# First weight unit issued from ScalarE's queue, and the input stream loaded in five parts

## What is computed

```
def _rmsnorm(x, g):
    xf = x.astype(jnp.float32)
    y = xf * lax.rsqrt(jnp.mean(xf * xf, axis=-1, keepdims=True) + EPS)
    return (y * g.astype(jnp.float32)).astype(x.dtype)

def _swiglu(xn, w_gate, w_up, w_down):
    return (jax.nn.silu(xn @ w_gate) * (xn @ w_up)) @ w_down
...
        f = _swiglu(_rmsnorm(h, ffn1_pre_g[i]), ffn1_w_gate[i], ffn1_w_up[i], ffn1_w_down[i])
        h = h + 0.5 * _rmsnorm(f, ffn1_post_g[i])
```

## Time and profile before

| | |
|---|---|
| time, median of 3 runs | 1560.12 us (1559.92 to 1560.37) |
| time of the profiled execution | 1560.24 us |
| its span, first to last instruction | 1558.5 us |
| TensorE busy with matmuls | 1546.3 us, 99% of the span |
| VectorE, ScalarE, GpSimd busy | 755.6, 597.5, 155.6 us |
| mean granted TensorE clock | 0.999 |
| bytes moved by DMA | 145.12 MB, mean 93 GB/s |

### The profile page before, as it was taken

How to read it: one execution, slowest core, us unless ns; L and a number is a source line. 1 busy time by engine, 2 the same in 40 slices (tenths; PEclk the granted TensorE clock), 3 DMA queues, 4 the chain that set the end, 5 groups by cost and what they waited for, 6 DMA issues and landing times.

```text
span 1558.5 us, 19025 instructions
## 1 busy us (share of the span) xinstructions
PE 1546.3 (99%) x7782; PEld 1276.9 (82%) x7782; DVE 755.6 (48%) x1190; ACT 597.5 (38%) x956; POOL 155.6 (10%) x162
## 2 busy tenths in 40 slices
PE   9999999999999999999999999999999999999998
PEld 7888888888888888888888888888888877777886
DVE  6444224346546633434843423333647455667545
ACT  6233222336433333324632323223656351544335
POOL 1311000101013400100111100110100010001100
PEclk9999999999999999999999999999999999999999
DMA  5433333322323322323233333333223452121322
GB/s 171 128 95 95 102 100 95 95 95 90 95 86 90 100 82 81 95 95 108 83 95 101 101 95 95 95 95 100 90 75 86 99 113 54 43 54 49 128 81 95
DMA packets 123735, 145.12 MB, mean 93 GB/s; under 512 B 18776, under 2 KB 86496, under 8 KB 123648
## 3 DMA queue, kind: packets, MB, share of 16 engines
q1 hardware_dynamic: 122080, 138.56, 29.5%
q0 software_dynamic: 1568, 5.34, 1.3%
HBM read 141.78 MB, written 2.10 MB: 92 GB/s over the span
## 4 chain that ended last, share of the span: by engine, by line
PE 96%; DVE 2%; ACT 1%; issue 0%; DMA 0%; POOL 0%; ACTq 0%; POOLq 0%; DVEq 0%
PE G L58 87%; PE X L58 6%; PE X L61 2%; PE G L61 1%; ACT sq_t L64 0%; DVE prb L76 0%; DVE f L70 0%; ACT prb L64 0%; DMA raw<-in_w_in_dram 0%; ACT whi L64 0%; DVE xl L73 0%; DVE ptr L67 0%; DVE h L73 0%; ACT post L64 0%; DVE tmp_t L70 0%
## 5 line engine op out<-in xcount | busy, mean ns | idle before, releaser
L70 DVE TENSOR_TENSOR wlo<-raw,whi 128x1024 fp32r<-128x1024 f32 (+3 forms) x261 | 313.2, 1209 | 490.1 <-ACT whi L64 489.9
L58 PE MATMUL G<-xh,whi 128*128 128x512 f32 (+1 forms) x1168 | 455.7, 392 | 0.2 <-DVE f L70 0.2
L58 PE MATMUL G<-xl,whi 128*128 128x512 f32 (+1 forms) x1168 | 449.9, 387 | 0.2 <-DVE xl L73 0.2
L58 PE MATMUL G<-xh,wlo 128*128 128x512 f32 (+1 forms) x1168 | 449.5, 386 | 0.4 <-DVE wlo L70 0.4
L64 ACT ACTIVATE whi<-raw 128x1024 fp32r<-128x1024 f32 (+3 forms) x261 | 266.3, 1031 | 459.2 <-DMA raw<-in_ffn_w_up_dram 159.3
L58 PEld LDWEIGHTS G<-xl,whi 128*128 128x128 f32 x1168 | 219.3, 188 | 45.5 <-DVE xl L73 0.6
L58 PEld LDWEIGHTS G<-xh,whi 128*128 128x128 f32 x1168 | 219.2, 188 | 44.1 <-issue 1.4
L58 PEld LDWEIGHTS G<-xh,wlo 128*128 128x128 f32 x1168 | 219.5, 188 | 43.2 <-DVE wlo L70 0.9
L70 POOL TENSOR_TENSOR tmp_t<-tmp_t,act_t 128x512 f32<-128x512 f32 x52 | 72.3, 1392 | 612.6 <-DVE tmp_t L70 472.1
L58 PE MATMUL G<-whi,ah 128*128 128x512 f32 x320 | 124.6, 389 | 0.0
L58 PE MATMUL G<-whi,al 128*128 128x512 f32 x320 | 124.5, 389 | 0.0
(11 more groups left out here) (272 smaller groups left out, 1795.8 us busy)
## 6 DMA issues: line engine op xcount, KB each, us to landing
raw<-in_w_in_dram SPq DMA_DIRECT2D x55, 512.0 KB, 3.7
raw<-in_ffn_w_gate_dram SPq DMA_DIRECT2D x88, 256.0 KB, 2.9
raw<-in_ffn_w_up_dram SPq DMA_DIRECT2D x88, 256.0 KB, 3.1
raw<-in_ffn_w_down_dram SPq DMA_DIRECT2D x44, 512.0 KB, 3.7
raw<-in_w_in_dram SPq DMA_DIRECT2D x12, 384.0 KB, 3.2
raw<-in_w_out_a_dram SPq DMA_DIRECT2D x8, 512.0 KB, 3.8
raw<-in_w_out_b_dram SPq DMA_DIRECT2D x8, 512.0 KB, 3.7
raw<-in_w_o_dram SPq DMA_DIRECT2D x8, 512.0 KB, 3.8
```

Of the source, the lines that this page charges most:

```text
L58: return self.e.matmul(out, lhs, rhs, start=start, stop=stop) if self.e else Idle()
L70: return self.e.tensor_tensor(*a) if self.e else Idle()
```

## The change

The first weight unit's two transfers are issued by ScalarE, as the first thing it does, with a signal of their own. `x` comes in five parts: channels 0 to 127, 128 to 255, and then three of 256. SyncE issues the first part of `x` ahead of the gain rows, and the wait for that part now stands behind the gain rows. Units 1 and 2 follow the third and the fourth part. TensorE transposes block 1 after the first four products of block 0, and blocks 2 and 3 after the first four products of block 1. VectorE and ScalarE take their steps in an order that fits this.

```
+        raw_first = signal("raw_first")
+        x_in = [signal(f"x_in{i}") for i in range(5)]
...
+        X_CUTS = (0, 128, 256, 512, 768, 1024)
+        X_PART = (0, 1, 2, 2, 3, 3, 4, 4)
...
+                            if (u, wi) in hooks and xv is hi:
+                                hooks[u, wi]()
                         if kk:
                             t.then_inc(*unit_read.event(n))
-                        else:
-                            hooks[2 * (u // 2), "half"]()
+                        elif (u, "half") in hooks:
+                            hooks[u, "half"]()
...
-                pe.wait_ge(x_in[k // 2], "x")
+                pe.wait_ge(x_in[X_PART[k]], "x")
...
             turn(0)
-            turn(1)
             fill(3)
             hooks = pre_hooks("s0")
-            hooks[0, "half"] = lambda: (turn(2), turn(3))
+            hooks[0, 0] = lambda: turn(1)
+            hooks[1, 0] = lambda: (turn(2), turn(3))
...
+            got, nk, wid = units[0]
+            v = raw[:, 0, 0:nk * wid].rearrange("p (k c) -> p k c", k=nk)
+            for p0, p1, k0, n, o, c, src in got:
+                act.dma_start(v[p0:p1, k0:k0 + n, o:o + c], src).then_inc(*raw_first.event(0, 16))
...
-                act.wait_ge(raw_in[n], n)
+                act.wait_ge(raw_in[n] if n else raw_first, n)
...
             split_half(0, 0)
+            split_half(0, 1)
             start_hi(1)
-            split_half(0, 1)
...
-            turn(1)
             dve.wait_ge(x_hi, ("x0", 0))
             turn(0)
             split_half(0, 0)
             dve.wait_ge(h_done, ("x0", 0))
             start_lo(0)
+            turn(1)
+            split_half(0, 1)
             start_lo(1)
-            split_half(0, 1)
...
-            sp.dma_start(rows[0:8, :], A["ffn1_pre_g"][0].rearrange("(a c) -> a c", c=128)).then_inc(*g_in.event("g", 16))
-            for n in range(4):
-                sp.dma_start(xrow[:, :, n * 256:(n + 1) * 256],
-                             A["x"][0].rearrange("(i p) c -> p i c", p=128)[:, :, n * 256:(n + 1) * 256]).then_inc(*x_in[n].event("x", 16))
-                if n < 3:
-                    send(n)
+            for n in range(5):
+                c = slice(X_CUTS[n], X_CUTS[n + 1])
+                sp.dma_start(xrow[:, :, c], A["x"][0].rearrange("(i p) c -> p i c", p=128)[:, :, c]).then_inc(*x_in[n].event("x", 16))
                 if n == 0:
+                    sp.dma_start(rows[0:8, :], A["ffn1_pre_g"][0].rearrange("(a c) -> a c", c=128)).then_inc(*g_in.event("g", 16))
                     sp.wait_ge(x_in[0], "x")
+                if n in (2, 3):
+                    send(n - 1)
```

More of the change, by code:

```diff
@@ L237, in two_blocks @@
         raw_in = [signal(f"raw_in{i}") for i in range(SLOTS)]
-        x_in = [signal(f"x_in{i}") for i in range(4)]
+        raw_first = signal("raw_first")
+        x_in = [signal(f"x_in{i}") for i in range(5)]
         g_in, row_in, gain_in = signal("g_in"), signal("row_in"), signal("gain_in")
```

## The result

The changed kernel takes 1562.32 us in the median of 22 runs (1561.93 to 1563.18), the kernel before 1560.09 us in the same runs (22 of them, 1559.47 to 1560.52). The ratio is 1.0015, with a 95% interval of 1.001 to 1.0021: slower by 2.2 us, 0.15%. It is outside the range I gave, which ended at 1562.0. The profiled execution took 1562.06 us with a span of 1560.3 us, against 1560.24 and 1558.5.

What follows compares the result with a forecast made beforehand. TensorE bounds the kernel, so only its start can pay, where gain rows and `x` end together. With R = 3.7 the mark moves +0.66 us: 1560.24 + 0.66 = 1560.9, less 0.12 for the median, 1560.8 us; range 1559.7 to 1562.0.

Steps and rivals of the forecast that it cites:

- R: Time at which TensorE can transpose the gain rows at the start: 3.7 us, range 3.5 to 4.2, against 2.74 before.
- the upper end of the bound: Gain rows landing only after 512 KB of `x` and weights: 0.81 + 3.4 = 4.2 us, sum +1.2 us.
- the mark: Start of block 0's `xh*wlo` products on TensorE: predicted 9.44 us against 8.78, so the rest moves by +0.66.
- The 0.41 us stall: TensorE's wait before block 0's `wlo` products, predicted to go and be replaced by 0.40 us of transposes.
- `xh` of block 1: Input of block 1's products: ready at R + 7.3, wanted by TensorE at R + 7.55, covered by 0.2 us only.
- ScalarE's table load and its two issues: At the start on ScalarE: the issues cost nothing; the load moves to 4.3 and ends at 5.6, ahead of `xh`.
- What the new order gives back: Block 1's transposes after block 0's first four products replace the stall before `wlo`: about 0.3 us returned.
- The change doesn't do what it says: Rival: the first `x` part lands no earlier because unit 0 runs beside it; R = 4.6, 1561.7 us; chance 0.05.
- the clock rival: Rival: TensorE's idle break delays its pace rise, 0.9 us per group of four products; one group 1561.7; chance 0.1.
- Early rows: Rival: the gain rows slip through beside the `x` part, R = 3.2, 1559.8 to 1560.3 us; chance 0.15.
- the second part of `x` is late: Rival: TensorE waits for it behind four products; if it took 6 us, 0.8 us stall, 1561.6; chance 0.05.
- The sign of the change: Whole kernel, told apart beyond about 0.2% (3.1 us): faster 0.01, same 0.95, slower 0.04.

Runs made afterwards that it cites:

- the last experiment: The changed kernel with the gain rows issued first on ScalarE's queue, ahead of unit 0, instead of on SyncE's behind `x`: 1559.99 us.
- the second profile of the kernel with the fills ahead: Repeat of the changed kernel with `fill(4)` moved ahead of the wait for the gain rows, run for another profile: 1563.01 us.
- the first profile: First profiled execution of the changed kernel with `fill(4)` moved ahead of the wait for the gain rows: 1560.77 us, against a median of 1562.45.

## Why the prediction was wrong

**The step that failed is R**, the time at which TensorE can transpose the gain rows. I took R = 3.7, from "a gate transfer of 256 KB, with another 256 KB right behind it, takes 2.9 us". It was 5.05. That row describes a transfer with a neighbour behind it in the same queue, and as such it is right: with one queue, `x` took 2.8 us and R was 3.60. The change puts the neighbour beside it, from the first moment, and with it `x` took 4.1 us and the gain rows behind it landed at 5.01. I also drew the upper end of the bound too low. I took "the landing of 512 KB", 3.4 us, as the worst that sharing could do, but beside the 256 KB of `x` lay 512 KB of unit 0, and all 768 KB had to move before `x` was surely complete. At the 347 GB/s of the earlier trace rows that is 2.3 us of moving against 1.5 for 512 KB, 0.8 us more than 3.4: 4.2 us, R = 5.0. I had the rate, and did not work this out.

These are the changed kernel's stretches (us; busy us of PE, PEld, DVE, ACT, POOL; PEclk, DMA share, GB/s):

```profile
2.00:3.00 1.00, 0.81 (x4) 0.51 (x3) 0.00 (x0) 0.00 (x0) 0.00 (x0) 1.00 0.74 178
3.00:4.00 1.00, 0.00 (x0) 0.00 (x0) 0.00 (x0) 0.00 (x0) 0.00 (x0) 1.00 1.04 341
4.00:5.00 1.00, 0.00 (x0) 0.00 (x0) 0.00 (x0) 0.00 (x0) 0.00 (x0) 1.00 0.76 262
5.00:6.00 1.00, 0.94 (x4) 0.92 (x5) 0.17 (x1) 0.39 (x1) 0.00 (x0) 1.00 0.01 3
```

178 + 341 + 262 is some 780 thousand bytes in three microseconds, nearly all of the 790 thousand of `x`, unit 0 and the gain rows, and then nothing, since SyncE waits for `x` before it asks for more. With the earlier trace rows at 347 GB/s, the trace agrees with the rule of the Trainium skill that I weighed ("DMA: Bandwidth & Descriptors", Rules for kernel authors): two issuing engines moved no more per microsecond than one. What that rule does not say is who is served first. The same page (Queues, rings and completion order) says that a DMA engine takes turns between the queues it has work for, packet by packet. If a turn holds as many rows of the one queue as of the other, which is an assumption of mine, the 512 rows of `x` at 512 bytes would end about with the 512 rows of unit 0 at 1 KB. The landings fit, `x` at 4.9 and the last of unit 0 at 5.4. They fit equal shares by bytes less well: by these `x` would be through when 512 KB have moved, at the 4.2 that I had as the upper end. But no run here varied the rows by themselves, so the turn-taking is argued and not shown.

**The steps that held.** From the gain rows to the first product I had 4.44 us, and it is 4.43 (5.05 to 9.48). From R to the mark I had 5.74, and it is 5.81: the first four products stand 1.03 us ahead of the next transpose, and not 0.90. The 0.41 us stall is gone. `xh` of block 1 is ready 0.2 us before TensorE wants it, as counted (ScalarE ends it at 12.59, the products start at 12.80). ScalarE's table load and its two issues cost nothing. With R = 5.05 the sum would have given +2.0 us, 1562.1. What the new order gives back, 0.3 us, was 0.22 in the changed kernel (1.38 us from the first product to the mark instead of 1.60), and 0.22 again in the last experiment, whose first product stands at 7.17 and whose mark at 8.56.

**The rivals.** "The change doesn't do what it says" came nearest: `x` landed at 4.92, later than the 4.64 of before. I had given it 0.05, with R = 4.6 and 1561.7. I had made its price from the old landing, as if sharing could at most undo the gain. The late pace of the clock rival is real, and 0.9 us for a group was about right: in the second profile of the kernel with the fills ahead the first group lost 0.85 (1.88 us to the next transpose instead of 1.03). But in the changed kernel the pace rose near 9 us instead of 6.4 (the identity passes at 7.97 still take 1.29 us for six), and in the profiled execution no product was hit. Its condition, that the break brings it about, is not shown. "Early rows" and "the second part of `x` is late" did not happen: that part landed 2.8 us after its issue at 4.92, at 7.7, and was wanted at 10.5.

**The sign of the change.** That the difference is slower and under 0.2% was in the forecast; its size, 2.2 us, was three times what I said.

## What to carry to other kernels

A small load that gates the start belongs ahead of the large one, or on another queue where nothing is ahead of it; behind a large transfer it waits for that transfer, here 3.7 us from issue to landing for 4 KB. A second queue moved no more bytes per microsecond here (341 against 347 GB/s), but it put the two transfers beside each other. To let one of them go first, hold the other back a little, here by 0.64 us. To bound a landing, add up all bytes that are asked for in the same stretch, on all queues, divide by the rate that the trace shows, and add what a small load takes by itself. With the 1.93 us of the gain rows and 341 GB/s this estimate gives 2.7 us for 256 KB alone, 3.5 for 512 KB and 4.2 for 768 KB, where the traces have 2.7 to 2.8, 3.4 and 4.1.

## What the runs showed of the hardware

Between two executions of the same kernel TensorE's pace in the first 12 us can differ by a factor of nearly two, while the granted clock reads 1.00 (the 2.4 GHz level) in all those stretches. In the second profile of the kernel with the fills ahead (1563.01 us) four products take 2.08 us, and its stretch reads:

```profile
8.00:12.00 4.00, 3.59 (x11) 2.90 (x12) 2.51 (x5) 0.88 (x2) 0.00 (x0) 1.00 0.98 311
```

In the first profile they take 1.20 us. The column does not tell these apart, the durations do. How far the executions of a kernel scatter differs a good deal: 1.0 us for the kernel before and for the one with one queue, 1.25 for the changed kernel, 2.2 and 2.3 for gain rows first and for TensorE kept busy, 3.1 where the fills were all moved ahead. It does not simply follow the length of the break: the changed kernel has the longest one.

Nor does it take a break. With one queue and gain rows first, and in the last experiment, TensorE has the same passes at the same times, to 0.02 us, from 1.59 to 4.81. Behind that, the first has

```profile
4.81 0.89 PE L61 MATMUL X<-ident,f 128*128 128x128 f32 x4
5.54 0.83 PE L58 MATMUL G<-ident 128*128 128x128 f32 x6
```

and the second

```profile
4.81 1.06 PE L61 MATMUL X<-ident,f 128*128 128x128 f32 x4
5.67 1.49 PE L58 MATMUL G<-ident 128*128 128x128 f32 x6
```

So in the first the pace rose during these transposes, and in the second only after these passes, over a microsecond later. When the pace rises, and why, was not isolated.

The other surprise is how much a head start is worth. Unit 0 issued at 0.80 instead of 1.45, on the same queue, beside the same `x` part, delayed `x` by 1.4 us.
